# Low parts of the block products: another order on GpSimd, one hold moved, product copies moved from VectorE to ScalarE

## The reference

```
h = rmsnorm(x);  q,k,v,latent,gates = h @ w_in
y_a, y_b = two attentions, projected
mix = (sigmoid(gate_a) * y_a + sigmoid(gate_b) * y_b) @ w_out      # 1024 x 1024
x = x + rmsnorm(mix)
u = rmsnorm(x) @ w_up; causal conv of width 3
f = (gelu(gate) * val) @ w_down                                     # 2816 x 1024
x = x + rmsnorm(f);  x = x + sigmoid(x @ w_ple_gate) * (p @ w_ple_proj)
```

## Time and profile before

| what | value |
|---|---|
| median of 3 runs | 1813.55 us (1813.34 to 1813.96) |
| the profiled execution's own time | 1813.86 us |
| its span | 1812.0 us |
| PE busy | 1796.0 us, 99% |
| DVE busy | 1169.2 us, 65% |
| POOL busy | 1105.0 us, 61% |
| ACT busy | 778.1 us, 43% |
| granted TensorE clock | full in all 40 slices |

### The profile page before, as it was taken

The page is one execution under the profiler, slowest core; times in us unless marked ns, Lnnn a source line. Parts: engine busy times, 40 slices in busy tenths (PEclk is TensorE's granted clock), DMA queues, the critical chain, the costliest instruction groups (busy, mean ns, idle before and its releaser), DMA issues.

```text
span 1812.0 us, 34936 instructions
## 1 busy us (share of the span) xinstructions
PE 1796.0 (99%) x13958; PEld 1736.5 (96%) x13958; DVE 1169.2 (65%) x2036; ACT 778.1 (43%) x1585; POOL 1105.0 (61%) x1364
## 2 busy tenths in 40 slices
PE   9999999999999999999999999999999999999999
PEld 8998989999999999999999988899999999999999
DVE  6677675445778568554657767753657795785554
ACT  4444453235556245332344444532365552552321
POOL 8676634548555845957666865345475558459384
PEclk9999999999999999999999999999999999999999
DMA  5342211324222222323342421122242223223232
GB/s 186 96 120 80 77 42 59 105 94 146 77 87 93 94 84 92 96 75 101 106 144 91 139 77 59 56 74 82 89 148 82 82 94 94 94 85 103 73 94 97
DMA packets 76465, 170.55 MB, mean 94 GB/s; under 512 B 6608, under 2 KB 34384, under 8 KB 76304
## 3 DMA queue, kind: packets, MB, share of 16 engines
q1 hardware_dynamic: 68976, 160.79, 28.0%
q10 hardware_dynamic: 7328, 7.54, 1.3%
HBM read 156.41 MB, written 9.79 MB: 92 GB/s over the span
## 4 chain that ended last, share of the span: by engine, by line
PE 88%; DVE 8%; ACT 1%; issue 1%; POOL 1%; DMA 0%; SPq 0%; DVEq 0%; POOLq 0%; ACTq 0%
PE ps L2153 56%; PE ps L2557 9%; PE ps L2193 4%; PE ps L2643 3%; PE ps L2321 3%; PE ps L2279 2%; PE ps L2576 1%; DVE R L1483 1%; PE ps L2232 1%; PE ps L2375 1%; PE ps L2381 1%; DVE xn L1483 1%; DVE RF L1785 1%; PE ps L2593 1%; PE ps L2298 1%
## 5 line engine op out<-in xcount | busy, mean ns | idle before, releaser
L2153 PE MATMUL ps<-xn,wsp 128*128 128x272 f32 x7728 | 989.8, 289 | 2.6 <-ACT R L1127 0.8
L2153 PEld LDWEIGHTS ps<-xn,wsp 128*128 128x128 f32 x7728 | 973.9, 189 | 8.0 <-issue 3.0
L836 POOL TENSOR_TENSOR wsp<-raw,wsp 128x256 fp32r<-128x256 f32 x440 | 346.4, 809 | 17.6
L822 POOL TENSOR_TENSOR wsp<-raw,wsp 128x256 fp32r<-128x256 f32 x216 | 158.8, 769 | 178.3 <-ACT wsp L1012 178.3
L831 POOL CAST wsp<-raw 128x512 fp32r<-128x512 f32 x220 | 151.6, 689 | 179.8 <-DMA raw<-in_wstream 124.1
L1483 DVE SCALAR_TENSOR_TENSOR R<-ps,R 128x512 fp32r<-128x512 f32 (+13 forms) x272 | 129.5, 499 | 64.6 <-ACT R L931 19.0
L810 POOL TENSOR_TENSOR wsp<-raw,wsp 128x512 fp32r<-128x512 f32 x80 | 121.9, 1545 | 67.4 <-DVE raw L1785 43.1
L817 POOL TENSOR_TENSOR wsp<-raw,wsp 128x256 fp32r<-128x256 f32 x136 | 100.9, 775 | 83.0 <-ACT wsp L1012 83.0
L2153 PE MATMUL ps<-R,wsp 128*128 128x272 f32 x960 | 124.8, 290 | 0.1
L2153 PEld LDWEIGHTS ps<-R,wsp 128*128 128x128 f32 x960 | 121.7, 189 | 1.4 <-DVE xT L1512 0.5
L2557 PE MATMUL ps<-R,wsp 128*128 128x272 f32 x816 | 110.3, 290 | 2.7 <-POOL wsp L810 2.5
(11 more groups left out here) (304 smaller groups left out, 2728.1 us busy)
## 6 DMA issues: line engine op xcount, KB each, us to landing
raw<-in_wstream SPq DMA_DIRECT2D x233, 512.0 KB, 3.6
raw<-in_wstream SPq DMA_DIRECT2D x48, 128.0 KB, 2.6
raw<-in_wstream SPq DMA_DIRECT2D x16, 384.0 KB, 3.2
xT<-in_x_in SPq DMA_DIRECT2D x16, 272.0 KB, 4.3
raw<-in_kc SPq DMA_DIRECT2D x8, 512.0 KB, 3.5
raw<-in_vc SPq DMA_DIRECT2D x8, 512.0 KB, 4.5
out_k_out<-mix ACTq DMA_DIRECT2D x8, 272.0 KB, 3.0
out_y_out<-xT ACTq DMA_DIRECT2D x1, 2176.0 KB, 9.6
```

The source lines that it names most:

```text
L822: ins = nc.gpsimd.tensor_tensor(dst[:, 1, f], part[:, f], dst[:, 0, f].bitcast(F32), ALU.subtract)
L836: ins = nc.gpsimd.tensor_tensor(dst[:, 1, f], part[:, f], dst[:, 0, f].bitcast(F32), ALU.subtract)
L2153: mm = pe.matmul(z[:, h], w[:, x, (k0 + k) * P:(k0 + k + 1) * P], rhs[:, y, k, h * HT:(h + 1) * HT], start=(k == 0 and (x, y) == (0, 0)), ...
```

## The change

The order of the six low parts becomes A11, S1, A22, S2, A12, S3 in all ten pairs. The wait of the first `w_out` pair for the last mix tile stands before S1 and no longer before A11. In part 0 of `w_down` ScalarE keeps P5, P2 and P4 as in `w_out`, and VectorE only joins P7 and P3, each with one addition; part 1 stays as it was, with one more wait for ScalarE's reads. All hand-ons now also wait for ScalarE's own earlier reads.

```
-DOWN_LOWS = ("A11", "S1", "S2", "A12", "S3", "A22")
+DOWN_LOWS = ("A11", "S1", "A22", "S2", "A12", "S3")

-            if t[0] in ("P2", "P4", "P5") and t[1] == OUT:
+            if t[0] in ("P2", "P4", "P5") and t[1] in (OUT, 0):
                 return 1, 0

-                            if (i, j) == (OUT, 0):
-                                pool.wait_ge(S["mi_lo"], M_LO[KT - 1, "B"])
                             for n in DOWN_LOWS:
+                                if (i, j) == (OUT, 0) and n == "S1":
+                                    pool.wait_ge(S["mi_lo"], M_LO[KT - 1, "B"])
                                 pool.wait_ge(pre["sum_hi"], highs_made(layer, i, j, n))

+                    def keep_product(i, n, j, m, h=0):
+                        act.wait_ge(S["p_done"], AT[(n, i, j)] + 1)
+                        ac(fT[:, m, h * HT:(h + 1) * HT], bank((n, i, j))[:, 0:HT], ACT.Copy).then_inc(S["act_read"], 1)
...
                         for j in range(1, NP) if covered else ():
                             hand_on(i, j, "P1", "P2")
                             if j < NP - 1:
                                 plain_high(i, j + 1)
+                            if i == 0:
+                                keep_product(0, "P5", j, j, 1)
                             hand_on(i, j, "P6", "P3")
+                            if i == 0:
+                                keep_product(0, "P2", j, j)
...
                             hand_on(i, j, "P7", "P4")
                             if j < NP - 1:
                                 sum_high(i, j + 1, "S4")
+                            if i == 0:
+                                keep_product(0, "P4", j, j + NP)

+                    def join_products(i, n, j, m, five):
+                        t = (n, i, j)
+                        dve.wait_ge(S["p_done"], AT[t] + 1)
+                        dve.wait_ge(S["act_read"], aread(t if n == "P7" else ("P5", i, j)))
+                        v.tensor_tensor(fT[:, m, HT:T], bank(t)[:, 0:HT], fT[:, five, HT:T], ALU.add).then_inc(S["dve_read"], 1)
...
-                            collect(i, "P5", j, ((j + NP, 1), (j, 1)), True)
+                            if i > 0:
+                                collect(i, "P5", j, ((j + NP, 1), (j, 1)))
...
-                            collect(i, "P2", j, ((j, 0),), True)
-                            collect(i, "P7", j, ((j + NP, 1),), False)
-                            collect(i, "P3", j, ((j, 1),), False)
+                            if i == 0:
+                                join_products(0, "P7", j, j + NP, j)
+                                join_products(0, "P3", j, j, j)
```

More of the change, by code:

```diff
@@ L1231, in hand_on @@
                         act.wait_ge(S["dve_read"], max(dread(o) for o in BEFORE[(to, i, j)]))
-                        if i == OUT:
-                            act.wait_ge(S["act_read"], max(aread(o) for o in BEFORE[(to, i, j)]))
+                        act.wait_ge(S["act_read"], max(aread(o) for o in BEFORE[(to, i, j)]))
                         act.wait_ge(S["p_done"], AT[(n, i, j)] + 1)
                         ac(bank((to, i, j))[:, 0:HT], bank(("P7", i, j))[:, 0:HT], ACT.Copy).then_inc(S["act_read"], 1)
+                    def keep_product(i, n, j, m, h=0):
+                        act.wait_ge(S["p_done"], AT[(n, i, j)] + 1)
+                        ac(fT[:, m, h * HT:(h + 1) * HT], bank((n, i, j))[:, 0:HT], ACT.Copy).then_inc(S["act_read"], 1)
                     for n, j in MIXES:
@@ L1269, in _ @@
                             hand_on(OUT, j, "P1", "P2")
-                        keep_product("P5", j, a, 1)
+                        keep_product(OUT, "P5", j, a, 1)
                         hand_on(OUT, j, "P6", "P3")
                         cast(("out", OUT_PLAIN[j]))
-                        keep_product("P2", j, a)
+                        keep_product(OUT, "P2", j, a)
                         hand_on(OUT, j, "P7", "P4")
@@ L1281, in _ @@
                             cast(("out", KT - 1))
-                        keep_product("P4", j, b)
+                        keep_product(OUT, "P4", j, b)
                         act.wait_ge(S["act_read"], aread(("P4", OUT, j)))
@@ L1381, in _ @@
                             if j == end and covered:
+                                if i == 0:
+                                    keep_product(0, "P5", 0, 0, 1)
                                 hand_on(i, 0, "P6", "P3")
@@ L1385, in _ @@
                                 sum_high(i, 1, "S2")
+                                if i == 0:
+                                    keep_product(0, "P2", 0, 0)
                                 hand_on(i, 0, "P7", "P4")
@@ L1390, in _ @@
                                 sum_high(i, 1, "S4")
+                                if i == 0:
+                                    keep_product(0, "P4", 0, NP)
                         for j in range(1, NP) if covered else ():
@@ L1792, in last_low, with collect @@
                                                ALU.mult, ALU.subtract).then_inc(pre["sum_raw"], 1)
-                    def collect(i, n, j, places, new):
+                    def collect(i, n, j, places):
                         t = (n, i, j)
@@ L1801, in collect @@
                             f, z = fT[:, m, h * HT:(h + 1) * HT], bank(t)[:, 0:HT]
[L1802 to L1805, removed]
+                            ins = v.tensor_tensor(f, z, f, ALU.add)
                         ins.then_inc(S["dve_read"], 1)
+                    def join_products(i, n, j, m, five):
[3 more added lines that the diff above has]
+                        v.tensor_tensor(fT[:, m, HT:T], bank(t)[:, 0:HT], fT[:, five, HT:T], ALU.add).then_inc(S["dve_read"], 1)
                     def gated_a(j):
@@ L1878, in _ @@
                     last_low(OUT, 0)
[L1879 to L1884, removed]
                     for j, (a, b) in enumerate(BLOCK_PAIRS[OUT]):
                         add_squares(0, 3 * j)
-                        join_products("P7", j, b, a)
-                        join_products("P3", j, a, a)
+                        join_products(OUT, "P7", j, b, a)
+                        join_products(OUT, "P3", j, a, a)
                         if j < len(BLOCK_PAIRS[OUT]) - 1:
@@ L2052, in _ @@
                                 dve.wait_ge(S["dve_read"], dread(("P4", i - 1, j)))
+                                dve.wait_ge(S["act_read"], aread(("P4", i - 1, j)))
                             if j == 1:
@@ L2061, in _ @@
                                     weight_sum(i, j + 1, n)
-                            dve.wait_ge(S["dve_read"], dread(("P5", i, j)))
-                            collect(i, "P2", j, ((j, 0),), True)
-                            collect(i, "P7", j, ((j + NP, 1),), False)
-                            collect(i, "P3", j, ((j, 1),), False)
+                            if i == 0:
+                                join_products(0, "P7", j, j + NP, j)
+                                join_products(0, "P3", j, j, j)
+                            else:
+                                dve.wait_ge(S["dve_read"], dread(("P5", i, j)))
+                                collect(i, "P2", j, ((j, 0),))
+                                collect(i, "P7", j, ((j + NP, 1),))
+                                collect(i, "P3", j, ((j, 1),))
                             if 0 < j < NP - 1:
                                 weight_sum(i, j + 1, "S4")
-                            collect(i, "P4", j, ((j + NP, 0),), True)
+                            if i > 0:
+                                collect(i, "P4", j, ((j + NP, 0),))
                             if j < NP - 1:
```

3 lines of the change are left out of this document (removed).

## The result

The changed kernel takes 1816.3 us, median of 22 runs (1816.1 of the 21 in the ratio), against 1813.7 us of 22 runs before: a ratio of 1.0013, 95% interval 1.0007 to 1.0019. The forecast was no change, 1813.4 us; it is slower by about 2.5 us, inside the range. Two executions of kernels with the moved hold, the profiled one of the changed kernel among them, took 6.1 to 6.2 ms, in that one with matmuls 0.44 us apart and not 0.13; they stand in no ratio, and nothing here explains them. So the profile shown is that of the same changed kernel run again (1816.38 us, 11 runs; profiled execution 1816.01 us, span 1814.2).

What follows compares the result with a forecast made beforehand. TensorE, busy nearly all the span, bounds the kernel; only 5.4 us of gaps can be won. Per layer -0.2 (w_out), -0.5 (part 0) and +0.65 (part 1) sum to about 0: 1813.4 us, range 1810.4 to 1816.6.

Steps and rivals of the forecast that it cites:

- The mechanism that held: First w_out pair: VectorE's addition at 407.38 stands until GpSimd's A11 low part ends, finishing at 408.8 instead of 408.10.
- my 414.9: First w_out pair: S2's low part ends at 414.85 instead of 414.18, so P6 waits until 414.9.
- The step that failed: First w_out pair: P6 waits for S2's low part; of 1.4 us removed, 1.2 return as waits of P6 and P7.
- the sum's term: w_out's first pair: -0.2 us per layer, bounds -0.8 and +0.2.
- Part 0: Part 0 of w_down: copies leave VectorE, P6 of pair 2 gains nothing, P4 starts earlier; -0.5 us per layer.
- Part 1: Part 1 of w_down: A22 before S2 makes P6 of pair 2 0.75 us late; +0.65 us per layer.
- (a): Part of the gain stays: VectorE's addition isn't held, A22 fits GpSimd's pause; -1.4 us per layer, 1810.7 us, chance 0.18.
- (b): Every gap in the three stretches closes, or nearly; -2.3 us per layer, 1808.9 us, chance 0.12.
- (d): w_out: second low part is held as the first was, P1's 1.4 us become P6's wait; no chance given.
- (c): Slower: A22 before S2 decides everywhere; +1.8 us per layer, 1817.1 us; chance 0.18 including what lies towards the forecast.

Runs made afterwards that it cites:

- the hold alone: Kernel before, with only the wait for the last mix tile moved from A11 to S1, old order of low parts: 1817.30 us, ratio 1.0017.
- the hand-on earlier: ScalarE's hand-on of P1 put ahead of its last mix high part: 1811.49 us with old order and moved wait, 1812.80 us on the changed kernel.
- hand-on later: Kernel before, with ScalarE's high parts of S3 and S4 of the first w_out pair cut into eight pieces each: 1816.81 us, ratio 1.0016.

## Why the prediction was wrong

**The mechanism that held.** VectorE's addition was held as forecast (1.38 us instead of 0.72), and all behind it came about 0.7 later. The Trainium skill has a rule for this (SBUF — State Buffer, section "Who interferes with whom"): a VectorE instruction with two inputs in SBUF contends with a GpSimd instruction that reads SBUF. The row agrees, 1.38 against 0.72 us. P1's wait went, and S2's low part ended at 414.05 in a kernel whose out 0 began 0.8 us earlier than before: relative to it that is my 414.9.

**The step that failed is what P6 waits for in `w_out`.** The prediction lets P6 wait for S2's low part, "P6 waits until 414.9; it started at [...] 415.23 before", and names "ScalarE's hand-ons, now later by the same 0.7" as a bound of +0.2, for P7 alone. But in the kernel before P6 came right behind P5 in one row of matmuls and its start was worked out by division, so its releaser was never read. P6 was already at the hand-on's limit. These are ScalarE's rows of the kernel before:

```profile
413.07 0.66 ACT L1210 ACTIVATE xn<-RF 128x544 fp32r<-128x544 f32 x1 [3.95 <-DVE RF L1834]
414.79 0.38 ACT L1235 ACTIVATE ps<-ps 128x272 f32<-128x272 f32 x1
```

The hand-on ended at 415.17 and P6's first matmul started at 415.27, 0.17 us after P5's last where the usual step is 0.13: P5 and the hand-on came to an end within 0.1 us of each other. The hand-on stands behind a high part that hangs on VectorE's held addition. When that moved by 0.7, hand-on and P6 moved by it: +0.64 us per layer in place of -0.2. With the hand-on taken out of that queue the sum's term comes out as written (-0.18).

**A term that the sum did not have: the clock.** Before, P1 stood 1.24 us and P6 came under 0.1 us late; with the hold moved P1 stands none and P6 2.05 us, in one pause. The order alone loses as much in `w_out` (41.70 us against 41.48), but in several pauses, the longest 1.24, and its clock was 1.0 in all 11. After the pause of 2.05 us, in layer 1 of the profiled execution (PE, timeline, then windows):

```profile
1314.51 1.89 PE L2572 MATMUL ps<-R 128*128 128x272 f32 x12 [2.05 <-issue]
1316.19 4.57 PE L2572 MATMUL ps<-xn,wsp 128*128 128x272 f32 x24
```

```profile
1312.00:1314.50 2.50, 0.46 (x4) 1.00 0.84 303
1314.50:1316.00 1.50, 1.49 (x12) 0.97 0.04 15
1316.00:1319.00 3.00, 3.00 (x15) 0.50 0.00 0
1319.00:1321.00 2.00, 2.00 (x17) 0.92 0.46 102
```

The clock is at 1.2 GHz instead of 2.4 for some 3.4 us, 24 matmuls take 4.57 us where 3.16 is usual, and the stretch is 1.5 us longer than in layer 0 with the hold alone (43.03 against 41.49), and 2.1 in the changed kernel, of which 0.5 is the last point below. A spell in one layer is 0.001 of the span's mean clock, so the 0.998, 0.999 and 1.0 of the changed kernel's executions read as two spells, one and none. Without a spell the terms are +0.64 - 0.66 + 0.48 = +0.46 us per layer, 1814.6 us; the four executions at 1.0 took 1813.4 to 1814.7. The 1.7 us from there to the median are about the size of one spell; how they divide between spells and the last point below is not shown.

**Part 0** was -0.66 to -0.71 for -0.5. Mechanism and sign were right, the split wrong: ScalarE's copies give 1.34 to 1.40, not the 1.1 written before that run, and the order costs 0.7 of it, at pair 1's hand-on and not behind S2 in pair 2. There one of the new copies (587.31) also stands in front of the hand-on, for which the prediction had counted over 0.1 us to spare. The prediction had also said that taking the copies away frees none of the shared port's time; VectorE's own time was enough, for without them sum S4 of pair 2 starts 1.9 us earlier in the stretch (20.73 against 22.61 us) and S2's low part 1.5.

**Part 1** was +0.48 for +0.65; the order alone gives the same +0.48. By the starts of the products the loss is spread over pairs 1 and 2 in steps of 0.1 to 0.2 us, not one wait of 0.75 in pair 2. That S2's low part of pair 2 ended where the working had it (at 737.79, which is 738.59 when the stretch's start is laid on that of the profile before, against 738.7) is luck: A22's low part started 0.8 us earlier than in the working and took 1.75 us, not the 1.1 given to it there.

**Of the rivals**, (a) and (b) fell. (d) came true in half: P1's wait did turn into one of P6, but 0.64 us longer and by ScalarE's hand-on, not by GpSimd. (c) has the right side, and its 1817.1 us is near the measured time, but its terms +0.2, +0.3 and +1.3 are not the measured +0.64, -0.66 and +0.48, so that is luck. In `w_out` the order alone costs (+0.86). But with the hold moved the order adds nothing there in layer 0 (41.48 against 41.49 for the hold alone), so A22 before S2 did not decide everywhere, which is what (c) says.

**The last point, and what is open.** In layer 1 the changed kernel and the order alone spend another 0.5 us between P5 and P6 of `w_out`'s second pair, not in layer 0 and not with the hand-on earlier. By the rows it is the same wait a third time: the hand-on of P1 ends at 1333.05 in the changed kernel and at 1332.70 with the order alone, P6 starts 0.14 us after it in both, and ScalarE had stood 3.6 us for VectorE's additions. Why VectorE is later there in layer 1 alone was not tried.

## What to carry to other kernels

Before you remove a wait, read for the next two products what releases each of them, even where no pause is printed: work out the end of every operation that it waits for, the one on the quiet engine (ScalarE, 43% busy here) included, and what that operation is queued behind. Several short pauses need not cost the same as one long one of their sum; ask what pause is left after the edit, not only how long all pauses are. And try a change's parts one by one: of three parts here one gained 2.5 us and two cost 3 us or more each, and together they came to +2.5 us, not to the sum of the three.

## What was new of the hardware

- TensorE's granted clock fell to 0.50 in or soon after a single pause of 2.05 us (the changed kernel, the hold alone; not in every execution) and of 2.66 us (all five executions), and stayed there some 3.4 us. With pauses of 1.24 us (before) the mean clock was 1.0 in 69 of 70 executions, and the one at 0.999 left no trace to say where it fell; with 1.24 and 1.19 us close together (hand-on later) it was 1.0 in all 11. The Trainium skill tells of this gate (TensorE: Matmul & The Clock Gate, section "Part 1: The HAM clock gate"): an idle TensorE runs at 1.2 GHz, and activity brings it to 2.4. The 0.50 behind the pauses agrees with that. That the same pause brings a spell in one execution and none in the next is what these runs add.
- A pause's label can name nobody or the wrong engine: "issue" for 2.05 us and GpSimd's `wsp` for 1.19 and 2.66 us stood where moving or delaying ScalarE's copy moved the start.
- A VectorE operation of 272 columns that takes 0.44 us alone took 1.52 and 1.53 us beside GpSimd again, and this reached TensorE by way of ScalarE.
- The prediction's words "one with a single SBUF input does not contend" are too wide. VectorE's copy `acc<-mix` (544 columns, one SBUF input) took 1.54 us beside GpSimd at 417.84 in the kernel before, and 0.43 at 417.69 in the changed kernel, where GpSimd rested. The copies that the change takes away read PSUM and took 0.43 us in all 32 cases.
